# The index heads' columns travel with x and are multiplied ahead of the first tile; the index keys' tile becomes stationary and its product is turned back

## What is computed

```python
h = x @ w_in                                   # 1024 -> 256 + 128 + 128 + 128 + 8
c_q, k, v, k_idx, w_idx = split(h)
c_q = rms_norm(c_q, g_cq)
q = c_q @ w_uq                                 # 16 heads of 64
q_idx = c_q @ w_iq                             # 8 index heads of 128
k_idx = layer_norm(k_idx, g_ik, b_ik)
q, k, q_idx, k_idx = rope(...)
w_idx = w_idx * (IDX_HEADS ** -0.5 * IDX_DIM ** -0.5)
rel = relu(einsum('bqhd,bsd->bhqs', q_idx, k_idx))
score = einsum('bqh,bhqs->bqs', w_idx, rel)    # top 64 keys of each token are kept
```

## Time and profile before

| | |
|---|---|
| median of 3 runs | 1049.61 us (1048.96 to 1050.8) |
| the profiled execution | 1049.57 us |
| its span, first to last instruction | 1047.7 us |
| busy: PE, PEld, DVE, ACT, POOL | 98%, 91%, 44%, 53%, 76% |
| chain that ended last, share of PE | 93% |
| mean granted TensorE clock | 0.998 |

### The profile page before, as it was taken

One profiled execution on the slowest core, in us unless ns is written; L12 is line 12 of the kernel. 1 busy time (PEld: TensorE's weight loads), 2 busy tenths in 40 slices (PEclk: granted clock), 3 DMA queues, 4 the chain that ended last, 5 costly groups with the idle time before them and its releaser, 6 DMA issues.

```text
span 1047.7 us, 17970 instructions
## 1 busy us (share of the span) xinstructions
PE 1027.8 (98%) x7744; PEld 950.0 (91%) x7744; DVE 464.3 (44%) x757; ACT 560.2 (53%) x779; POOL 794.0 (76%) x238
## 2 busy tenths in 40 slices
PE   7989999999999999999999999999999999999997
PEld 7868899998889997899998899999999988999986
DVE  4884263349824774445321142921253252533303
ACT  6784544443358775454444266466568356444420
POOL 4826898879678756889888779677674978988880
PEclk9999999999999999999999999999999999999999
DMA  9404655555545332765555356454443555555541
GB/s 361 155 2 173 229 196 186 187 195 201 187 178 198 123 121 83 252 249 190 185 191 198 128 196 235 167 187 151 177 170 105 218 201 184 198 202 187 185 151 40
DMA packets 27454, 186.59 MB, mean 178 GB/s; under 512 B 3168, under 2 KB 3424, under 8 KB 5872
## 3 DMA queue, kind: packets, MB, share of 16 engines
q1 hardware_dynamic: 25184, 178.83, 47.4%
q10 hardware_dynamic: 2192, 6.62, 1.8%
HBM read 184.39 MB, written 1.05 MB: 177 GB/s over the span
## 4 chain that ended last, share of the span: by engine, by line
PE 93%; ACT 2%; DVE 2%; POOL 1%; DMA 1%; issue 0%; DVEq 0%; SPq 0%; POOLq 0%
PE ps L416 86%; ACT arena L880 1%; PE ps L1535 1%; PE ps L1205 1%; DMA stage<-in_tiles 1%; PE ps L2249 1%; ACT arena L889 0%; POOL wl L393 0%; PE ps L766 0%; DVE arena L1093 0%; PE ps L2254 0%; PE ps L1553 0%; DVE arena L1088 0%; PE ps L1341 0%; PE ps L2266 0%
## 5 line engine op out<-in xcount | busy, mean ns | idle before, releaser
L393 POOL TENSOR_TENSOR wl<-stage,wh 128x2048 fp32r<-128x2048 f32 x165 | 762.1, 4640 | 209.1 <-ACT wh L389 189.0
L389 ACT ACTIVATE wh<-stage 128x2048 fp32r<-128x2048 f32 (+1 forms) x167 | 317.9, 1907 | 111.5 <-DMA stage<-in_tiles 110.7
L416 PE MATMUL ps<-xh,wh 128*128 128x256 f32 x1328 | 369.4, 278 | 1.4 <-DVE wl L542 1.4
L416 PE MATMUL ps<-xl,wh 128*128 128x256 f32 x1328 | 367.6, 277 | 0.0
L416 PE MATMUL ps<-xh,wl 128*128 128x256 f32 x1328 | 367.6, 277 | 0.0
L416 PEld LDWEIGHTS ps<-xh,wh 128*128 128x128 f32 x1328 | 249.4, 188 | 3.8 <-DVE wl L542 1.7
L416 PEld LDWEIGHTS ps<-xl,wh 128*128 128x128 f32 x1328 | 249.8, 188 | 0.1
L416 PEld LDWEIGHTS ps<-xh,wl 128*128 128x128 f32 x1328 | 249.6, 188 | 0.0
L416 PE MATMUL ps<-wh,xh 128*128 128x512 f32 (+2 forms) x400 | 134.6, 336 | 1.2 <-DVE xl L1142 0.9
L416 PE MATMUL ps<-wh,xl 128*128 128x512 f32 (+2 forms) x400 | 132.5, 331 | 0.0
L416 PE MATMUL ps<-wl,xh 128*128 128x512 f32 (+2 forms) x400 | 132.4, 331 | 0.0
(11 more groups left out here) (381 smaller groups left out, 1137.1 us busy)
## 6 DMA issues: line engine op xcount, KB each, us to landing
stage<-in_tiles SPq DMA_DIRECT2D x167, 1024.0 KB, 4.9
arena<-in_ln_g ACTq DMA_DIRECT2D x4, 512.0 KB, 3.9
arena<-in_ln_b ACTq DMA_DIRECT2D x4, 512.0 KB, 5.3
arena<-in_x_t SPq DMA_DIRECT2D x1, 1024.0 KB, 5.5
x_res<-in_x SPq DMA_DIRECT2D x1, 1024.0 KB, 20.9
out<-x_res SPq DMA_DIRECT2D x4, 256.0 KB, 2.0
stage<-in_tiles SPq DMA_DIRECT2D x1, 544.0 KB, 9.4
arena<-in_pre_mix_norm ACTq DMA_DIRECT2D x1, 512.0 KB, 7.2
```

The lines of the kernel that those rows point to most:

```text
L389: nc.scalar.activation(tile_of(wh, n, *part), tile_of(stage, n, *part), ACT.Copy).then_inc(hi_done, 1)
L393: nc.gpsimd.tensor_tensor(tile_of(wl, n), tile_of(stage, n), tile_of(wh, n).bitcast(F32), ALU.subtract).then_inc(lo_done, 1)
L416: last = mm(o, l, r, start=start and i == 0, stop=stop and i == 2, skip_group_check=skip)
```

## The change

The 8 columns of the index heads leave tile 1 and travel at the end of x's rows (64 columns more in `x_t`). ScalarE and VectorE split them first, and TensorE multiplies them by x, stationary with 8 columns, after 7 instead of 12 warm-up products and ahead of tile 0, as x's quarters come. VectorE copies the result `wi_t` (8 x 256) out of PSUM. Tile 1 has 128 columns a block; it is stationary now and x moves, so its product lies with the tokens along the free side. VectorE copies it to `ki_t`, and four transposes bring keys and heads back to where the code behind expects them. The squares of c_q are added in two halves by VectorE and summed over the partitions by half the products, between the two halves of the first `query`. On ScalarE the Sin comes ahead of the squares, under a table loaded at the start, and the copies of tiles 3, 4 and 5 are cut in halves and placed between other steps; `late_loads` (two transfers on ACT's queue) comes after tile 3. GpSimd's subtraction for tile 5 comes after its part of the attention.

```diff
-        x_raw = cut(0, KD, T)
+        x_in_t = cut(0, KD * (T + IH))
+        x_raw, heads_raw = x_in_t[:, 0:KD * T].rearrange("p (k t) -> p k t", k=KD), x_in_t[:, KD * T:KD * (T + IH)]
+        heads_h, heads_l = hh[:, 10, 0:KD * IH], hl[:, 10, 0:KD * IH]
+        ki_t, wi_t = cut(8704, T), cut(8960, T)[0:IH, :]
...
         def setup_dve(dve):
+            dve.wait_ge(heads_hi.sem, heads_hi.due(dve))
+            V.tensor_tensor(heads_l, heads_raw, heads_h.bitcast(F32), ALU.subtract).then_inc(heads_lo.sem, heads_lo.up())
             for c in range(4):
                 x_lo(dve, c, x_raw)
...
             dve.wait_ge(hi_done, 2)
-            first_low(1, (0, KD * IW))
+            first_low(1, (0, KD * ID))
+            dve.wait_ge(wi_ps.sem, wi_ps.due(dve))
+            V.tensor_copy(wi_t, ps[0:IH, 5, 0:T]).then_inc(wi_turned.sem, wi_turned.up())
...
         def setup_x_act(act):
-            nc.scalar.preload_act_table_set("natural_log_exp_and_others")
+            nc.scalar.preload_act_table_set("trig_and_small")
             setup_loads(act)
             act.wait_ge(xt_in, 16)
+            nc.scalar.activation(heads_h, heads_raw, ACT.Copy).then_inc(heads_hi.sem, heads_hi.up())
...
-            keep_warm(7, 12)
+            keep_warm(7, 7)
+            pe.wait_ge(heads_lo.sem, heads_lo.due(pe))
+            for c in range(4):
+                pe.wait_ge(x_ready.sem, x_ready.due(pe))
+                for k in range(2 * c, 2 * c + 2):
+                    w = slice(k * IH, (k + 1) * IH)
+                    last = mm3(ps[0:IH, 5, 0:T], (heads_h[:, w], heads_l[:, w]), (xh[:, k, :], xl[:, k, :]), k == 0, k == KD - 1)
+            last.then_inc(wi_ps.sem, wi_ps.up())
...
             low_ready(pe, 1)
+            for k in range(KD):
+                o = k * ID
+                last = mm3(ps[:, 4, 0:T], (tile_of(wh, 1, o, o + ID), tile_of(wl, 1, o, o + ID)),
+                           (xh[:, k, :], xl[:, k, :]), k == 0, k == KD - 1)
+            last.then_inc(used, 1)
+            pe.wait_ge(wi_turned.sem, wi_turned.due(pe))
+            pe.wait_ge(ki_copied.sem, ki_copied.due(pe))
             for t in range(2):
                 x = slice(t * P, (t + 1) * P)
-                for k in range(KD):
-                    o = k * IW
-                    last = mm3(ps[:, 1, t * T:t * T + IW], (xh[:, k, x], xl[:, k, x]),
-                               (tile_of(wh, 1, o, o + IW), tile_of(wl, 1, o, o + IW)), k == 0, k == KD - 1)
-            last.then_inc(used, 1)
-
-            def query(n, t, bank, first=None):
+                nc.tensor.transpose(ps[:, 1, t * T:t * T + ID], ki_t[:, x], ident[:])
+                last = nc.tensor.transpose(ps[:, 1, t * T + ID:t * T + IW], wi_t[:, x], ident[0:IH, 0:IH])
+            last.then_inc(ki_ps.sem, ki_ps.up())
+
+            def squares_summed():
+                pe.wait_ge(sq_sum.sem, sq_sum.due(pe))
+                for t in range(2):
+                    last = mm(ps[:, 3, t:t + 1], cqt[:, 0, t * P:(t + 1) * P], mean_hd[:, 0:1], start=True, stop=True)
+                last.then_inc(ss_ps.sem, ss_ps.up())
...
-            for t in range(2):
-                for k in range(2):
-                    last = mm(ps[:, 3, t:t + 1], cqt[:, k, t * P:(t + 1) * P], mean_hd[:, 0:1], start=k == 0, stop=k == 1)
-            last.then_inc(ss_ps.sem, ss_ps.up())
-            query(2, 1, (6, 7)).then_inc(iq_ps.sem, iq_ps.up())
+            query(2, 1, (6, 7), between=squares_summed).then_inc(iq_ps.sem, iq_ps.up())
...
-            hi_until(act, 3)
-            late_loads(act)
+            setup_act2(act)
+            nc.scalar.preload_act_table_set("natural_log_exp_and_others")
             act.wait_ge(cq_ready.sem, cq_ready.due(act))
...
-            setup_act2(act)
-            nc.scalar.preload_act_table_set("natural_log_exp_and_others")
...
+            hi_half(3, 0)
             act.wait_ge(ki_var.sem, ki_var.due(act))
...
-            hi_until(act, 5)
+            hi_half(3, 1)
+            late_loads(act)
+            hi_half(4, 0)
...
             index_plain(1)
             index_turned(1)
+            hi_half(4, 1)
...
             index_turned(0)
+            hi_half(5, 0)
...
+            hi_half(5, 1)
             hi_until(act, 7)
...
             dve.wait_ge(used, 2)
+            V.tensor_copy(ki_t, ps[:, 4, 0:T]).then_inc(ki_copied.sem, ki_copied.up())
+            dve.wait_ge(ki_ps.sem, ki_ps.due(dve))
...
             V.tensor_scalar(wi, bank2(1)[:, :, ID:IW], float(IH ** -0.5 * ID ** -0.5), None, ALU.mult)
+            dve.wait_ge(sq_done.sem, sq_done.due(dve))
+            V.tensor_tensor(cqt[:, 0, :], cqt[:, 0, :], cqt[:, 1, :], ALU.add).then_inc(sq_sum.sem, sq_sum.up())
...
-            for n in range(2, 6):
+            for n in range(2, 5):
                 lo(pool, n)
             dsa_pool(pool)
+            lo(pool, 5)
```

More of the change, by code:

```diff
@@ L113, in weight_tiles @@
     w_att = A["att_w_in"][0]
-    keys = w_att.reshape(KD, P, -1)[:, :, 512:648].transpose(1, 0, 2).reshape(P, -1)
+    keys = w_att.reshape(KD, P, -1)[:, :, 512:640].transpose(1, 0, 2).reshape(P, -1)
     columns(w_att, 0, 256)
-    tiles.append(np.concatenate([keys, np.zeros((P, TW - KD * IW), keys.dtype)], axis=1))
+    tiles.append(np.concatenate([keys, np.zeros((P, TW - KD * ID), keys.dtype)], axis=1))
     tiles.append(rows(A["att_w_iq"][0], 0, 2))
@@ L328, in build @@
         numbers, trig_done, reduced_t, trig_t_done = signals("numbers trig_done reduced_t trig_t_done")
-        first_hi, first_lo, wo_lo = signals("first_hi first_lo wo_lo")
+        first_hi, first_lo, wo_lo, sq_sum = signals("first_hi first_lo wo_lo sq_sum")
+        heads_hi, heads_lo, wi_ps, wi_turned, ki_copied, ki_ps = signals("heads_hi heads_lo wi_ps wi_turned ki_copied ki_ps")
         QUARTER = TW // 4
@@ L363, in build @@
             "rest", "gv", "gq", "gk", "gg", "gate", "uq", "ukv", "gwo", "mwo", "out", "ffn2"))
-        stationary = {0, *(t_hx + i for i, (x, j) in enumerate(HX) if x != "g"), *range(t_gq, t_ukv), *range(t_gwo, t_out),
+        stationary = {0, 1, *(t_hx + i for i, (x, j) in enumerate(HX) if x != "g"), *range(t_gq, t_ukv), *range(t_gwo, t_out),
                       *(base + f for base in (t_ffn0, t_ffn1, t_ffn2) for f in range(2 * BY_TOKEN, NF))}
-        moving = {1, 3, *(t_hx + i for i, (x, j) in enumerate(HX) if x == "g"), *range(t_rest, t_gq)}
+        moving = {3, *(t_hx + i for i, (x, j) in enumerate(HX) if x == "g"), *range(t_rest, t_gq)}
         SHIFT = [16 if n in stationary else 48 if n in moving else 0 for n in range(FIRST["end"])]
@@ L377, in load @@
             if n == 1:
-                sp.dma_start(tile_of(stage, 1, 0, KD * IW), A["tiles"][1, :, 0:KD * IW]).then_inc(stage_in[1], 16)
+                sp.dma_start(tile_of(stage, 1, 0, KD * ID), A["tiles"][1, :, 0:KD * ID]).then_inc(stage_in[1], 16)
                 return
@@ L387, in hi @@
             act.wait_ge(stage_in[ring(n)], come[n])
-            part = (0, KD * IW if n == 1 else TW)
+            part = (0, KD * ID if n == 1 else TW)
             nc.scalar.activation(tile_of(wh, n, *part), tile_of(stage, n, *part), ACT.Copy).then_inc(hi_done, 1)
@@ L699, in dsa_pe @@
             pe.wait_ge(consts.sem, consts.due(pe, 2))
-            keep_warm(7, 12)
+            keep_warm(7, 7)
[6 more added lines that the diff above has]
+            last.then_inc(wi_ps.sem, wi_ps.up())
             for c in range(4):
                 pe.wait_ge(first_lo.sem, c + 1)
-                pe.wait_ge(x_ready.sem, x_ready.due(pe))
                 for m in range(2):
@@ L710, in dsa_pe, with query @@
             low_ready(pe, 1)
+            for k in range(KD):
[5 more added lines that the diff above has]
+            pe.wait_ge(ki_copied.sem, ki_copied.due(pe))
             for t in range(2):
                 x = slice(t * P, (t + 1) * P)
-                for k in range(KD):
-                    o = k * IW
-                    last = mm3(ps[:, 1, t * T:t * T + IW], (xh[:, k, x], xl[:, k, x]),
-                               (tile_of(wh, 1, o, o + IW), tile_of(wl, 1, o, o + IW)), k == 0, k == KD - 1)
-            last.then_inc(used, 1)
-            def query(n, t, bank, first=None):
+                nc.tensor.transpose(ps[:, 1, t * T:t * T + ID], ki_t[:, x], ident[:])
[6 more added lines that the diff above has]
+                last.then_inc(ss_ps.sem, ss_ps.up())
+            def query(n, t, bank, first=None, between=None):
                 low_ready(pe, n)
@@ L728, in query @@
                         last.then_inc(first.sem, first.up())
+                    if between and c == 0:
+                        between()
                 return last
@@ L747, in dsa_pe @@
             pe.wait_ge(cq_ready.sem, cq_ready.due(pe))
-            pe.wait_ge(sq_done.sem, sq_done.due(pe))
-            for t in range(2):
-                for k in range(2):
-                    last = mm(ps[:, 3, t:t + 1], cqt[:, k, t * P:(t + 1) * P], mean_hd[:, 0:1], start=k == 0, stop=k == 1)
```

(19 more changed lines are left out.)

## The result

The changed kernel takes 1053.3 us (median of 6, 1052.75 to 1053.79) against 1049.28 for the kernel before in the same series: ratio 1.0037, 95% interval 1.0026 to 1.0047. It is slower by 4.0 us, where 1048.6, 1.0 us faster, was predicted. The profiled execution took 1053.79 us for a span of 1052.0.

What follows compares the result with a forecast made beforehand. TensorE was taken to bound the kernel, front gains before 51.53 arriving nearly whole; -1.82 + 0.55 + 0.27 = -1.00, so 1049.57 - 1.00 = 1048.6 us. Likeliest range 1048.0 to 1049.1; 8 in 10, 1047.2 to 1050.2.

Steps and rivals of the forecast that it cites:

- its part on ScalarE and POOL: Later copies and GpSimd order: halved copies fit idle spans, tile 5's low part finds idle POOL; late wait +0.27 us.
- Index keys' tile, transposed product: TensorE after tile 0: 24 products of 256 columns replace 48, taking 2.78 us, saving 2.54.
- Turning back: Between key products and index query: copy out of PSUM, four transposes holding TensorE 0.45 us; together +1.13.
- Squares: Between the first query's halves: four matrix rows replace eight, summed after VectorE's add; -0.86 + 0.45 = -0.41 us.
- Heads' products: 24 products ahead of tile 0, slow until the clock rises; they delay tile 0 by 0.1 to 1.0 us, taken +0.55.
- d: Delay of tile 0's first product against its start at 11.12 before: 0.1 to 1.0 us, taken as +0.55.
- Rival (a): TensorE's clock rises no earlier than the heads' end at 13.1: d = 2.0, time 1050.0 us; chance 0.15.
- First index rope: VectorE's first rope of the index query was to come 1.3 us earlier than 26.07.
- Late stage: Before the first logits: POOL's k rope falls 0.77 us behind through kr's later copy, costing +0.27, 0.77 at most.
- Table load: ScalarE's front: one load goes away, off the path; the load between Sin and squares takes 1.28 us.
- the drain that was weighed: About 1380 ns more after ScalarE's table load, by the skill; would give 1049.0 us; rejected for the trace.

Runs made afterwards that it cites:

- experiment 1: Changed kernel with GpSimd's low part of tile 6 held back behind the last normalisation: 1048.24 us, ratio 0.9992.
- experiment 2: Kernel before with only GpSimd's low part of tile 5 moved behind its part of the attention: 1053.8 us, ratio 1.0054.
- experiment 3: Changed kernel, GpSimd's order untouched, VectorE's products of the probabilities also writing an unread row sum: 1049.79 us, ratio 1.0004.
- experiment 5: On top of experiment 1, ScalarE's copy of tile 7 cut in halves, the second behind the first turned queries: 1047.98 us, ratio 0.9981.
- experiment 6: On top of experiment 1, warm-up started at about 1.5 us instead of 4.26, with 15 products instead of 7: 1047.83 us, ratio 0.998.
- experiment 4: Kernel before with GpSimd's low part of tile 6 held back behind the last normalisation, as a control: 1049.3 us, ratio 1.0003.

## Why the prediction was wrong

**The step that failed** is the last sentence of its part on ScalarE and POOL: "The low part of tile 5 moves on POOL from before its scores to after its ropes; it is first used behind the attention, with 19.79 us of idle POOL ahead of 75.89." It costed the move at nothing because the result isn't wanted early and the engine is free. Both are so; what it didn't ask is what VectorE does while GpSimd works there. Experiments 1 and 2 show that the move costs 4.7 to 5.1 us, more than the whole net loss, and experiment 3 that it does so by blocking one form of VectorE's instruction. The trace of before had it nearly in sight:

```profile
51.57 4.53 POOL L393 TENSOR_TENSOR wl<-stage,wh 128x2048 fp32r<-128x2048 f32 x1
```

```profile
55.96 1.01 DVE L922 TENSOR_SCALAR arena<-arena,small 128x128 f32<-128x128 f32 x4
```

Tile 6's part ended at 51.57 + 4.53 = 56.10 there, and the first four products started at 55.96; 4.5 us more of GpSimd could only land on them. The row with GpSimd's idle 19.79 us names VectorE's L922 as what ended it: GpSimd was idle there because the code makes it wait for the last normalisation.

The Trainium skill has the rule, and the prediction didn't weigh it for this edit: SBUF — State Buffer, section Who interferes with whom, says that VectorE in a two-port mode and GpSimd share one pair of ports by an exclusive lock for the whole instruction, that the second to issue fully blocks, and that `tensor_scalar` can enter such a mode but not the form that also writes its accumulator. Every part of this that the runs touch agrees: the first two products take 0.63 and 4.60 us and end with a GpSimd instruction each, none waits in experiment 3, and the operations that read PSUM don't.

**The other steps**, by their terms (the sum was -1.00; the trace after gives -0.52 at the first logits, 51.53 to 51.01):

- Index keys' tile, transposed product: 24 products from 17.13 to 19.85, 2.72 us against 2.78. Right.
- Turning back: 1.57 from that slot to the query at 21.42, against 1.13. The copy takes the 0.42 named; the four transposes hold TensorE for 0.80 (20.62 to 21.42) and not 0.45. Those of the heads (stationary 8 x 128, moving 8 x 8) alternate with full ones, and each pair takes about 0.4, where eight equal rows go 0.11 apart. Mis-sized by 0.44.
- Squares: from the query's start to the rope 25.13 - 21.42 = 3.71, before 26.07 - 22.86 = 3.21: +0.50 against +0.45. Right.
- Heads' products: tile 0 starts at 11.69, d = 0.57 against 0.55, with the slow rows first, as said. That the size fits so well is luck: in experiments 1 and 3 d is 0.36 and 0.17, and in 5 and 6 tile 0 starts at 10.99 and 10.65, ahead of the 11.12 of the earlier trace rows, which the prediction had excluded; experiment 2, with the front of before, starts it at 10.63. So 11.12 was one execution's arrival of tile 0's data and no bound. Rival (a), a clock that stays low into tile 0, is not what happened.
- First index rope: -0.94 against -1.27, the turn being the difference.
- Late stage: POOL's k rope waits 0.87 for kr, and the first logits come when the warm-up rows end: +0.42 against +0.27. Right in kind; experiment 5 removes it.
- Table load: the load of 18.42 takes 1.28 and the squares start at 19.71; they follow the load by 0.01, without the drain that was weighed.
- Two slips in the prediction's sums change nothing: 24 fast products from 7.8 end at 10.58 and not 10.4, and 51.53 less 1.00 puts the first logits at 50.5 and not 50.3.

With the one collision taken out, experiment 1 gives 1048.24, 0.4 below the predicted 1048.6. In kind the sum was right, and the list of what it summed was one short. That the number fits so well is in part luck: the turn and the late stage were priced 0.44 and 0.15 too low, and experiment 1's trace has the first logits only 0.76 ahead of before's. Another 0.54 of its profiled execution's lead lies behind the first product with w_o, 968.24 - 967.70 us, where the change does nothing.

## What to carry to other kernels

When work moves onto an idle stretch of GpSimd, read VectorE's timeline over that stretch, not only the moved work's due time. A plain `tensor_scalar` from SBUF to SBUF waited there for the end of a whole GpSimd instruction, 4.5 us for a 128x2048 subtraction, while operations that read PSUM didn't. An engine that a kernel keeps idle behind a wait that its own data don't need may be a sign of such a collision; find out what the wait protects before you count the idle time as room. And when a kernel's first products come slow although their data are there, try starting the warm-up earlier: from 1.5 us in place of 4.26 it took the slow products out of the trace (experiment 6), at a gain too small for these times to size.

## What the runs showed of the hardware

**Two GpSimd instructions in a row let one VectorE instruction through.** In the trace after, VectorE's first product ended with the first subtraction, and the second took 4.60 us, until the next subtraction was done. The wait that the first product sat out won nothing for those queued behind it.

**A subtraction of two SBUF tensors waits too.** The kernel before has such waits where the change does nothing. Here a feed-forward layer's split on VectorE meets a tile's on GpSimd:

```profile
228.05 4.61 POOL L393 TENSOR_TENSOR wl<-stage,wh 128x2048 fp32r<-128x2048 f32 x1 [2.25 <-ACT wh L389]
```

```profile
L1459 DVE TENSOR_TENSOR hl<-arena,hh x54: 425/1282/4641, 138.5 to 986.4; 128x256 fp32r<-128x256 f32 x54
```

The one at 228.31 takes 4.63 us. The 54 of this line, all of 128x256, take 425 ns at the least, 1282 in the median and 4641 at the most, while the same shape with one input in PSUM (L1474) takes 420 to 422 in all of its 54. The trace shows no other engine waiting for this line, so here these waits cost the kernel nothing that it shows, but the form with two SBUF inputs is to be looked for as well as the plain product.

**The clock can fall between the warm-up and tile 0.** In experiment 4, whose front is that of the kernel before, TensorE warmed up from 4.26 until 8.63, idled until 10.88, and then had this (windows as above, granted clock third from the end):

```profile
5.00:8.60 3.60, 3.60 (x23) 3.44 (x21) 1.38 (x3) 2.04 (x4) 0.00 (x0) 1.00 0.99 394
8.60:10.90 2.30, 0.06 (x2) 0.02 (x1) 1.89 (x4) 1.58 (x4) 0.00 (x0) 0.96 1.05 415
10.90:14.00 3.10, 3.10 (x14) 3.10 (x15) 3.04 (x5) 2.22 (x4) 0.00 (x0) 0.50 1.02 428
14.00:20.00 6.00, 6.00 (x55) 6.00 (x54) 3.62 (x15) 3.25 (x4) 4.46 (x1) 0.99 1.00 422
```

The first products of tile 0, until about 14, ran 0.21 apart, at the 1.2 GHz level, and the first logits came at 52.82 instead of 51.53. In the trace of before TensorE idled there for only 1.38 us, from 9.74 to 11.12, and tile 0 ran fast. The kernel before spreads over 2.4 us in the first series and 4.1 in the second, experiments 2 and 4, with its front, over 3.1 and 3.0, and the versions with the heads' products in that gap over 1.0 to 2.0. That fits, though the kernel before was also run more often (27 and 25 times against 6 to 11). No second trace with a slow tile 0 was taken, so the link to the spread is argued and not shown.
